# A pooling stage between two MLPs: channel mixing before the neighbour means, and the means as banded products on TensorE

## The reference, cut to what matters

```python
a = _modulate(_rmsnorm(h, norm1_g[1]), shift, scale)      # y * (1 + scale) + shift
# _multiscale_pool(a, w, pool_scale): 4 groups of 256 channels, windows of 2, 4, 8 and 16 tokens
for g, win in enumerate((2, 4, 8, 16)):
    lo, hi = clip(t - win // 2, 0, 512), clip(t + win - win // 2, 0, 512)
    mean = (cumsum[hi] - cumsum[lo]) / (hi - lo)
    outs.append(mean - a[..., 256 * g:256 * (g + 1)])
y = einsum("blgc,gcd->blgd", outs, w) * pool_scale        # a 256 x 256 matrix for each group
h = h + gate * y
```

## Time and profile before

| what | value |
|---|---|
| median of 3 runs | 2615.61 us |
| the profiled execution | 2618.41 us |
| its span | 2616.6 us |
| granted TensorE clock, mean over the span | 0.954 |
| TensorE matmul busy | 2375.1 us |
| VectorE busy | 1032.2 us |
| ScalarE busy | 622.2 us |
| GpSimd busy | 129.2 us |

### The profile page before, as it was taken

How to read it: one execution, slowest core, us unless ns; L and a number is a source line. 1 busy time by engine, 2 the same in 40 slices (tenths; PEclk the granted TensorE clock), 3 DMA queues, 4 the chain that set the end, 5 groups by cost and what they waited for, 6 DMA issues and landing times.

```text
span 2616.6 us, 23468 instructions
## 1 busy us (share of the span) xinstructions
PE 2375.1 (91%) x9809; PEld 1373.8 (53%) x9809; DVE 1032.2 (39%) x1633; ACT 622.2 (24%) x1000; POOL 129.2 (5%) x133
## 2 busy tenths in 40 slices
PE   5999988899999599999789989799898989899887
PEld 2446454588888378888666747433332323233222
DVE  4565462466654866665565362411011011101011
ACT  2112152323223242233345463310000000000000
POOL 2000000000000200000221312000000000000000
PEclk8999988999999799999899989899999999999999
DMA  9212320355552145552211202499999999999997
GB/s 349 104 65 81 135 91 0 113 193 191 180 192 97 44 148 176 183 180 74 84 53 33 93 29 104 182 427 430 431 431 429 431 431 430 431 430 431 431 430 317
DMA packets 121023, 594.18 MB, mean 227 GB/s; under 512 B 9346, under 2 KB 10880, under 8 KB 95190
## 3 DMA queue, kind: packets, MB, share of 16 engines
q1 hardware_dynamic: 117522, 583.23, 56.1%
q0 software_dynamic: 3088, 9.33, 1.0%
q10 hardware_dynamic: 308, 0.13, 0.0%
HBM read 590.54 MB, written 2.13 MB: 227 GB/s over the span
## 4 chain that ended last, share of the span: by engine, by line
PE 74%; DMA 13%; DVE 7%; ACT 3%; issue 1%; POOL 0%; ACTq 0%; DVEq 0%; POOLq 0%
PE PS L1150 15%; PE PS L865 9%; PE PS L867 9%; PE PS L866 9%; PE PS L681 7%; PE PS L891 5%; PE PS L149 5%; PE PS L1167 3%; DMA RB_a<-in_w_down_dram 2%; PE PS L1177 2%; PE PS L589 2%; DMA RB_a<-in_w_gate_dram 2%; DMA RING<-in_w_gate_dram 2%; DMA RING<-in_w_down_dram 2%; PE PS L765 2%; PE PS L616 1%
## 5 line engine op out<-in xcount | busy, mean ns | idle before, releaser
L1150 PE MATMUL PS<-RING,HID_e 128*64 128x512 f32 x608 | 208.7, 613 | 9.4 <-DMA RING<-in_w_gate_dram 5.4
L1150 PE MATMUL PS<-RB_a,HID_e 128*64 128x512 f32 x576 | 197.3, 601 | 8.6 <-DMA RB_a<-in_w_gate_dram 5.7
L1150 PE MATMUL PS<-HID_e 128*64 128x512 f32 x288 | 132.4, 608 | 3.8 <-DMA HID_e<-in_w_gate_dram 2.7
L1150 PE MATMUL PS<-AT_g,HID_e 128*64 128x512 f32 x288 | 130.7, 601 | 5.0 <-DMA AT_g<-in_w_up_dram 4.1
L1150 PE MATMUL PS<-XT,HID_e 128*64 128x512 f32 x288 | 130.5, 600 | 4.1 <-DMA XT<-in_w_gate_dram 2.6
L2458 DVE TENSOR_TENSOR TMP<-TMP,PS 128x512 f32<-128x512 f32 x32 | 19.9, 682 | 280.8 <-PE PS L1150 280.8
L1683 ACT ACTIVATE PADS<-PS 128x512 f32<-128x512 f32 x8 | 4.8, 597 | 495.0 <-PE PS L149 495.0
L1167 PE MATMUL PS<-RB_a,HID_e 128*64 128x512 f32 x304 | 107.1, 625 | 12.9 <-DMA RB_a<-in_w_down_dram 12.9
L2466 DVE TENSOR_TENSOR HID_e<-PS,HID_e 128x512 f32<-128x512 f32 x16 | 10.3, 686 | 272.0 <-PE PS L1167 272.0
L1167 PE MATMUL PS<-RING,HID_e 128*64 128x512 f32 x288 | 104.7, 621 | 12.0 <-DMA RING<-in_w_down_dram 12.0
L1150 PEld LDWEIGHTS PS<-RING,HID_e 128*64 128x64 f32 x608 | 62.6, 140 | 96.7 <-issue 83.6
(11 more groups left out here) (449 smaller groups left out, 4729.9 us busy)
## 6 DMA issues: line engine op xcount, KB each, us to landing
RING<-in_w_gate_dram SPq DMA_DIRECT2D x19, 2048.0 KB, 22.1
RING<-in_w_up_dram SPq DMA_DIRECT2D x19, 2048.0 KB, 17.0
RB_a<-in_w_down_dram SPq DMA_DIRECT2D x19, 2048.0 KB, 21.8
RB_a<-in_w_gate_dram SPq DMA_DIRECT2D x18, 2048.0 KB, 22.7
RB_a<-in_w_up_dram SPq DMA_DIRECT2D x18, 2048.0 KB, 17.6
RING<-in_w_down_dram SPq DMA_DIRECT2D x18, 2048.0 KB, 21.8
RING<-in_mlp_w_dram SPq DMA_DIRECT2D x32, 1024.0 KB, 5.8
RB_a<-in_mlp_w_dram SPq DMA_DIRECT2D x32, 1024.0 KB, 5.5
```

Source lines behind the costliest of these rows:

```text
L1150: last = pe.matmul(b[64 * d:64 * d + 64, :], xv_[:, k, 64 * d:64 * d + 64], wv, start=k == 0, stop=k == 7)
```

## The change

The stage is computed in another order. Mixing channels and averaging tokens commute, and so does the norm's factor 1/rms, which belongs to a token.

1. ScalarE multiplies the group weights by the norm's gain (`gained`), after its last split of MLP 0. The gains themselves are formed by VectorE at block 27 of MLP 0.
2. TensorE multiplies the residuals, not normed, with the gained weights: tokens come out on the partitions, a group's 256 channels on the columns. It also forms the shift's product with the weights, the same row on all partitions (`shifted`).
3. VectorE reads each product once: times the token's 1/rms (here a column, so that norm 3 needs no spread), plus the shift row. The result is `pooled`.
4. TensorE multiplies `pooled` with the banded matrix "mean of the window minus the token" of the group. A tile of 128 tokens reaches 144 columns at most; the 16 columns that two tiles share are written by a matmul of their own. The result has channels on partitions, as `XT`.
5. The table of the bands (864 KB) takes the place of the 1/count table, and is requested after block 27 of MLP 0. GpSimd has no windows any more.
6. VectorE's first split of MLP 1 stands ahead of the adds to `XT`, the second behind norm 4. ScalarE's first split waits for MLP 0's last matmul only. The group weights' ring slot is free after the shift products and the gains.

```diff
-        inv = H(0, hid=HID2)
-        wide = HID2[:, 2048:2048 + 12 * 528].rearrange("p (k n) -> p k n", k=12)
+        gained = AT2[:, 0:4, :].rearrange("p a b -> p (a b)").rearrange("p (k n) -> p k n", k=8)
+        band = AT2[:, 4:8, :].rearrange("p a b -> p (a b)")[:, 0:1728].rearrange("p (g c n) -> p g c n", g=4, c=3)
+        shifted = CAT2[:, 0:2, :].rearrange("p a b -> p (a b)")
+        pooled = HID2[:, 0:4096].rearrange("p (t n) -> p t n", t=4)
...
             ring.load(sp, w, ("pool",), A["pool_w"][0].rearrange("g (k p) n -> p (g k) n", p=128), (8, 256),
-                      (T_pool, "mm", 7))
+                      (T_pool, "shift", 1), (S_pool, "gain", 7))
...
-            w.wait_ge(*V_mlp.at("add", 0, 3, 7))
-            w.wait_ge(*T_mlp.at("mm", 0, 31, 3))
-            pool.dma_start(inv, K["invcnt"].rearrange("(o a) n -> o a n", o=1).to_broadcast([128, 4, 512])).then_inc(
-                *D["inv"].up())
...
-            for k in (5, 7):
-                w.wait_ge(*S_nrm.at("out", 3, k))
-                w.wait_ge(*G_pool.at("zero", 1))
-                pool_window(pool, w, G_pool, k)
+            w.wait_ge(*T_mlp.at("mm", 0, 27, 3))
+            pool.dma_start(band, K["band"]).then_inc(*D["band"].up())
...
         def pe_pool(pe, w):
-            pe_norm(pe, w, 3, 512)
+            def products(g):
+                for half in range(2):
+                    b = banks.take(w, ("pool_in", g, half), (V_pool, "in", g, 2 * half + 1))
+                    for i in (2 * half, 2 * half + 1):
+                        for k in (2 * g, 2 * g + 1):
+                            w.wait_ge(*S_pool.at("gain", k))
+                            w.wait_ge(*V_mlp.at("add", 0, 3, k))
+                            last = pe.matmul(b[:, 256 * (i % 2):256 * (i % 2) + 256], XT[:, k, i * 128:(i + 1) * 128],
+                                             gained[:, k, :], start=k % 2 == 0, stop=k % 2 == 1)
+                    last.then_inc(*T_pool.up("in", g, half))
+
+            w.wait_ge(*ring.landed("pool"))
+            w.wait_ge(*V_ada.at("add", 1, 1))
+            for hf in range(2):
+                b = banks.take(w, ("pool_shift", hf), (S_pool, "shift", hf))
+                for k in range(4 * hf, 4 * hf + 4):
+                    o = 256 * (k // 2 % 2)
+                    last = pe.matmul(b[:, o:o + 256], mod1[:, k:k + 1].to_broadcast([128, 128]), ring.view("pool")[:, k, :],
+                                     start=k % 2 == 0, stop=k % 2 == 1)
+                last.then_inc(*T_pool.up("shift", hf))
+            products(0)
+            products(1)
+            pe_norm_cols(pe, w, 3, 512, (S_nrm, "root", 3))
+            products(2)
+            products(3)
+            w.wait_ge(*D["band"].all())
             for jj in range(8):
-                g, j = jj // 2, jj % 2
                 b = banks.take(w, ("pool", jj), (V_pool, "add", jj))
...
+                w.wait_ge(*V_pool.at("in", jj // 2, 3))
+                for i in range(4):
+                    t0, t1 = max(0, 128 * i - 8), min(512, 128 * i + 136)
+                    for a, z in ((t0, t0 + 16), (t0 + 16, t1)) if i else ((t0, t1),):
+                        last = pe.matmul(b[:, a:z], pooled[:, i, jj * 128:(jj + 1) * 128],
+                                         band[:, jj // 2, (i + 1) // 2, a - t0:z - t0], start=z - a > 16,
+                                         stop=z - a == 16 or i == 3)
...
+        def act_pool(act, w):
+            w.wait_ge(*V_pool.at("g", 2))
+            w.wait_ge(*ring.landed("pool"))
+            w.wait_ge(*T_mlp.at("mm", 0, 27, 3))
+            for k in range(8):
+                act.activation(gained[:, k, :], ring.view("pool")[:, k, :], ACT.Identity, bias=0.0,
+                               scale=g1s1[:, k:k + 1]).then_inc(*S_pool.up("gain", k))
+            act_norm_squares(act, w, 3, lambda k: XT[:, k, :], 512, lambda k: V_mlp.at("add", 0, 3, k))
+            for hf in range(2):
+                w.wait_ge(*T_pool.at("shift", hf))
+                act.activation(shifted[:, 512 * hf:512 * hf + 512], banks.of("pool_shift", hf), ACT.Copy, bias=0.0,
+                               scale=1.0).then_inc(*S_pool.up("shift", hf))
+            act_norm_sqrt(act, w, 3, 512)
...
         def dve_pool(dve, w):
             dve_norm_sum(dve, w, 3, 7)
...
+            w.wait_ge(*S_nrm.at("root", 3))
+            dve.reciprocal(norm_col(3, 4, 4), norm_col(3, 0, 4)).then_inc(*V_nrm.up("recip", 3))
+            w.wait_ge(*S_pool.at("shift", 1))
+            w.wait_ge(*V_nrm.at("recip", 3))
+            for g in range(4):
+                for i in range(4):
+                    w.wait_ge(*T_pool.at("in", g, i // 2))
+                    dve.scalar_tensor_tensor(out=pooled[:, i, 256 * g:256 * g + 256],
+                                             in0=banks.of("pool_in", g, i // 2)[:, 256 * (i % 2):256 * (i % 2) + 256],
+                                             scalar=norm_col(3, 4 + i), in1=shifted[:, 256 * g:256 * g + 256],
+                                             op0=ALU.mult, op1=ALU.add).then_inc(*V_pool.up("in", g, i))
+            dve_split(dve, w, 1, 0)
...
             dve_pool(dve, w)
-            dve_split(dve, w, 1, 0)
+            dve_norm_split(dve, w, 4, ffns[1][0], ffns[1][1])
             dve_split(dve, w, 1, 1)
-            dve_norm_split(dve, w, 4, ffns[1][0], ffns[1][1])
```

More of the change, by code:

```diff
@@ L210, in build_program @@
         T_mlp, S_mlp, V_mlp = signal("pe_mlp"), signal("act_mlp"), signal("dve_mlp")
-        T_pool, V_pool, G_pool = signal("pe_pool"), signal("dve_pool"), signal("pool_pool")
+        T_pool, S_pool, V_pool = signal("pe_pool"), signal("act_pool"), signal("dve_pool")
         T_ml, S_ml, V_ml, G_ml = signal("pe_mlstm"), signal("act_mlstm"), signal("dve_mlstm"), signal("pool_mlstm")
@@ L216, in build_program @@
         D = {n: signal(f"landed_{n}", 16) for n in
-             ("id", "fw", "cm", "x", "dft", "rope", "brow", "inv", "rb", "scr", "bg", "blk", "tri", "br", "out", "wr",
+             ("id", "fw", "cm", "x", "dft", "rope", "brow", "band", "rb", "scr", "bg", "blk", "tri", "br", "out", "wr",
               "vec0", "vec1", "vec2", "gb0", "gb1", "gb2", "gb3")}
@@ L492, in gpsimd_program @@
                            K["rope"].rearrange("a p n -> p a n")).then_inc(*D["rope"].up())
-            w.wait_ge(*V_mlp.at("add", 0, 3, 7))
-            w.wait_ge(*T_mlp.at("mm", 0, 31, 3))
-            pool.dma_start(inv, K["invcnt"].rearrange("(o a) n -> o a n", o=1).to_broadcast([128, 4, 512])).then_inc(
-                *D["inv"].up())
-            pool.memset(wide[:, 0:8, 0:8], 0.0).then_inc(*G_pool.up("zero", 0))
-            pool.memset(wide[:, 0:8, 520:528], 0.0).then_inc(*G_pool.up("zero", 1))
-            w.wait_ge(*D["inv"].all())
-            for k in (5, 7):
-                w.wait_ge(*S_nrm.at("out", 3, k))
-                w.wait_ge(*G_pool.at("zero", 1))
-                pool_window(pool, w, G_pool, k)
+            w.wait_ge(*T_mlp.at("mm", 0, 27, 3))
+            pool.dma_start(band, K["band"]).then_inc(*D["band"].up())
             w.wait_ge(*T_mlp.at("mm", 1, 31, 3))
@@ L565, in pool_out2 @@
                 *G_out.up("lo", k))
[L567 to L583, removed]
         def transposes(pe, out, ins):
@@ L1448, in act_split @@
             else:
-                w.wait_ge(*V_pool.at("diff", 6))
-                w.wait_ge(*G_pool.at("diff", 7))
+                w.wait_ge(*T_mlp.at("mm", 0, 31, 3))
             act.activation(WH[:, jn % 2, :].rearrange("p (k n) -> p k n", n=512), ring.view("mlp", m, jn), ACT.Copy,
@@ L1746, in scalar_program @@
             act_mlp(act, w, 0)
-            act_norm_root(act, w, 3, lambda k: XT[:, k, :], 512, lambda k: V_mlp.at("add", 0, 3, k))
-            act_norm_out(act, w, 3, lambda k: wide[:, k, 8:520], 512, g1s1, mod1[:, 0:8], V_pool.at("g", 2),
-                         T_mlp.at("mm", 0, 31, 3))
+            act_pool(act, w)
             act_split(act, w, 1, 0)
@@ L2141, in dve_mlp @@
                     dve_ada(dve, w, 1 + m, s)
+                if m == 0 and s == 13:
+                    w.wait_ge(*V_ada.at("add", 1, 11))
+                    gain(dve, V_pool, ("g", 0), g1s1, mod1[:, 8:16], vc("norm1_g", 8, 8))
+                    dve.tensor_tensor(gps, mod1[:, 16:24], vc("pool_scale", 0, 8), ALU.mult).then_inc(*V_pool.up("g", 1))
+                    gain(dve, V_pool, ("g", 2), g2s1, mod1[:, 32:40], vc("norm2_g", 8, 8))
         def dve_pool(dve, w):
             dve_norm_sum(dve, w, 3, 7)
[L2145 to L2154, removed]
+            w.wait_ge(*S_nrm.at("root", 3))
[10 more added lines that the diff above has]
+            dve_split(dve, w, 1, 0)
             for jj in range(8):
@@ L2564, in constants @@
     c["rope"] = rope
-    ic = np.zeros((4, 512), f)
+    band = np.zeros((4, 512, 512), f)
     for g, w in enumerate((2, 4, 8, 16)):
@@ L2568, in constants @@
         hi = np.clip(t + w - w // 2, 0, 512)
-        ic[g] = f(1.0) / (hi - lo).astype(f)
```

(7 more changed lines are left out.)

## The result

The changed kernel took 2594.18 us, the median of 4 runs (2593.76 to 2595.18), beside 2614.51 us for the kernel before (the median of 4 runs now, one more than ahead of the prediction): a ratio of 0.9922 (0.9905 to 0.994), 20.3 us less. The forecast was 2594.8, from 2589 to 2604: both medians lie inside it.

What follows compares the result with a forecast made beforehand. The serial chain through the pool stage between the MLPs, 60.9 us, was taken as the bound. MLP 1 starting at 898.75 instead of 919.86, less 0.3 stall, saves 20.8 us: median 2594.8 us, range 2589 to 2604.

Steps and rivals of the forecast that it cites:

- column sums of norm 3: TensorE's sums for norm 3, placed behind the products of groups 0 and 1: 1.06 us, their input ready by then.
- bands: TensorE's banded window matmuls, 56 matmuls or 112 records at 0.112 us: 12.54 us at full clock.
- last band to last sum: Add, square and sum after the last band, taken as before the change: 2.3 us.
- sums to end of spread: Norm 4's column sums, root, reciprocal and spread of 1/rms: 3.4 us, with no VectorE splits before the reciprocal.
- spread to MLP 1: From the end of norm 4's spread to MLP 1's first matmul: 3.2 us, as before the change.
- stall in MLP 0's tail: The gains delay the last weight block's split in MLP 0, so TensorE stalls 0.3 us; ends 0 and 0.6.
- The price of a small matmul: In the bands, each record costs 0.112 us at full clock, whatever its width below 130 columns.
- rival 1: The clock falls in the bands, small records cost 0.224 us: 8.3 us saved, 2607.3 us; chance 0.12.
- The clock: TensorE's granted clock during the bands: unknown, taken as full (1.00), with columns needing 59% of the time.
- The waits: Between products and bands TensorE waits for nothing; reads 0.45 us each, late adds caught up at the eighth block, margin 0.4.
- The gains: ScalarE's 8 scalings of the group weights in MLP 0's tail: 3.7 us, against 3.4 us free.
- misread waits: Rival 4: a misread order of waits (a bank, late adds, second split) costs 5 to 15 us; chance 0.07.

Runs made afterwards that it cites:

- e3: Changed kernel with every block of bands computed twice into the same PSUM bank; median 2607.29 us, ratio 0.9964 to the kernel before.
- e11: Changed kernel with the bands cut into pieces of at most 16 columns, 288 matmuls for 56; 2702.2 us, ratio 1.0327 to the kernel before.
- e5: Changed kernel with ScalarE's and VectorE's first two weight splits of MLP 1 moved into the wait for norm 3's column sums; median 2593.69 us.
- e2: Changed kernel with ScalarE's 8 gain scalings of the group weights done twice, first into a spare buffer; median 2595.07 us.
- e4: Changed kernel without the shift rows: their 8 matmuls, 2 copies and the second operand of the reads removed; median 2589.78 us.
- e6: Changed kernel with unread 512-column matmuls in norm 4's gaps, 2 after the last band and 3 after the spread; median 2590.51 us.

## Why the prediction was right

The time came out by the steps that the prediction named, nearly term by term.

| step | predicted | measured |
|---|---|---|
| shift rows | 3.45 | 3.46 |
| products | 13.80 | 13.9 (6.90 + 7.01) |
| column sums of norm 3 | 1.06 | 0.79 |
| bands | 12.54 | 12.58 |
| last band to last sum | 2.3 | 2.4 |
| sums to end of spread | 3.4 | 3.5 |
| spread to MLP 1 | 3.2 | 3.2 |
| stall in MLP 0's tail | 0.3 | 0.09 |

**The price of a small matmul** was the step that carried most: 0.112 us for a record whatever its width below 130 columns, read from 129 and from 2 columns. It held for the mix of 16, 120, 128 and 136 columns (12.58 / 112 = 0.112), and twice over in e3 (0.113). At half clock e11's records took some 0.21 each (95 in 20 us), near the 0.224 of rival 1.

**The clock** was the open question, settled for full clock by the stretches that held. The chip agreed, and e3 and e11 show on which side the bands lie: in pieces of 16 to 136 columns, mixed and back to back, it held for 25 us; in pieces of at most 16 it fell after some 3.3 us.

**The waits.** The reads were 0.40 us apart rather than 0.45, and the last two waited for the last products; the adds began at 879.55, not 880.7 (by my own terms it should have read 880.5: the last two reads end at 877.3 + 0.9 = 878.2, not 878.4). They caught up at the third block, not the eighth: I had charged each of the first adds with a sum that the first two don't carry, and so put the margin at 0.4 us, which is too small. e5 shows that earlier adds are worth nothing. The split behind norm 4 ended at 910.3, and ScalarE was released by the end of block 0 at 912.2, a margin of 1.9 (1.5 predicted).

**The column sums** of norm 3 were the term of the stage furthest off, by 0.27 us: I took 1.06 us from sums that stood behind a wait. The same 8 records took 0.79 right behind other matmuls, and 1.04 behind a wait again, in norm 4.

**The gains** took 3.29 us against 3.7, still within the two ends. That their cover was nearly gone is what e2 shows.

**Where the median agrees by luck.** The stage gained 21.0 us, and the first pair of medians differ by 20.3, the second by 23.5. I took 2.8 us off for the difference between a profiled execution and the median; it says nothing about the change. In the one pair of profiles, 2.7 us lie in the attention, where the granted clock differed (0.88 and 1.00); that the medians differ for the same reason is not shown. That they agree with the forecast to 0.6 and 2.3 us is in part luck. The sum for the stage was good to 0.3 us; most of the range of 15 us stood for the clock in the bands and for misread waits (rivals 1 and 4).

## What to carry to other kernels

When TensorE waits for a stage of elementwise work, price the same sums as matmuls by the record, from the nearest widths in the trace, and look in the trace for what the granted clock did under matmuls of like width. Before moving work into the last blocks of a neighbour stage, follow the in-order queue behind it to the instruction that the critical engine waits for: the free 3.4 us here took one load of gains and not two. And look for algebra before scheduling: the shift of a normed layer falls out of "mean minus value", and dropping it was worth more than every reordering tried.

## What the runs showed of the hardware that I had not expected

- The second operand of a read cost nothing here: 128x256 from PSUM took 478 ns on VectorE with a column scalar and an added row, and 475 ns as a plain multiplication by the column (e4).
- 1.9 us of 512-column matmuls right after the bands (e6, 4 records) did not keep the clock: it was at 0.50 in 894 to 896, as in the changed kernel. The three after the spread had it at 0.79 in 896 to 898, where the changed kernel is at 0.50 until 902 and at 0.59 in 902 to 904.
- The same program begins the same stage at different times: the changed kernel at 858.2 and 859.3 us, the one without shift rows at 853.7 and 856.1. The granted clock in 310 to 345 us, far ahead of the stage, was 0.90, 0.90, 1.00 and 0.95 in these four profiles. For an effect of 1 us the length of the stage in the profile tells more than the median of four runs.
